# Third block of a decoder: compression, compressed scores, recurrence and convolution norm between the input projection's tiles

## What is computed

```
z = rms_norm(x) @ w_in            # 2848 columns: q, kc, vc, ks, vs, kw, vw, gates, conv, gla
kc, vc = compress(kc), compress(vc)     # 31 overlapping blocks of 32 tokens: silu(flat @ w1 + b1) @ w2
y_nsa  = g0*attn(q, kc, vc) + g1*attn(q, ks, vs) + g2*attn(q, kw, vw)      # 8 heads, 2 kv heads
y_conv = silu(layer_norm(causal depthwise conv of 31 taps (a * sigmoid(g))))
y_gla  = rms_norm(chunked gated linear attention (8 chunks of 64)) * silu(gr)
x = x + [y_nsa, y_conv, y_gla] @ w_out  # then feed-forward and embedding
```

## Time and profile before

| | |
|---|---|
| median of three executions | 2480.53 us (2477.56 to 2482.07) |
| the profiled execution, its own time | 2478.39 us |
| its span in the trace | 2476.6 us |
| PE, DVE, ACT, POOL busy | 2323.7, 1197.3, 913.4, 836.7 us |
| mean granted TensorE clock | 0.963 |

### The profile page before, as it was taken

How to read it: one execution, slowest core, us unless ns; L and a number is a source line. 1 busy time by engine, 2 the same in 40 slices (tenths; PEclk the granted TensorE clock), 3 DMA queues, 4 the chain that set the end, 5 groups by cost and what they waited for, 6 DMA issues and landing times.

```text
span 2476.6 us, 26005 instructions
## 1 busy us (share of the span) xinstructions
PE 2323.7 (94%) x10172; PEld 1784.8 (72%) x10172; DVE 1197.3 (48%) x2159; ACT 913.4 (37%) x1465; POOL 836.7 (34%) x328
## 2 busy tenths in 40 slices
PE   6999899999999899999999999999879899999997
PEld 4666678887877565557888878778774468888876
DVE  4444575553256565653655542447327553333124
ACT  3455443332233544543334322332217333222232
POOL 2222244444433111113444444344310034444442
PEclk9999999999999999999999999999759789999998
DMA  7111133333222101102332322253210023333222
GB/s 255 51 52 47 52 98 100 96 94 105 93 83 83 54 30 35 39 26 78 95 101 94 98 97 96 85 166 101 74 43 1 1 68 94 101 95 107 94 90 77
DMA packets 58347, 201.03 MB, mean 81 GB/s; under 512 B 6416, under 2 KB 10016, under 8 KB 58224
## 3 DMA queue, kind: packets, MB, share of 16 engines
q1 hardware_dynamic: 55360, 194.94, 24.8%
q10 hardware_dynamic: 2864, 4.40, 0.5%
HBM read 197.19 MB, written 7.38 MB: 83 GB/s over the span
## 4 chain that ended last, share of the span: by engine, by line
PE 81%; DVE 8%; ACT 6%; issue 2%; DMA 2%; SPq 0%; POOL 0%; ACTq 0%; DVEq 0%; PEldq 0%
PE lin L439 22%; PE lin L441 22%; PE lin L440 22%; PE lin L780 2%; DVE arena L1382 1%; PE scores L701 1%; PE obank L723 1%; PE turn L536 1%; ACT arena L1709 1%; PE lin L455 1%; PE obank L621 1%; PE lin L457 1%; PE lin L456 1%; PE scores L705 1%; PE scores L852 1%
## 5 line engine op out<-in xcount | busy, mean ns | idle before, releaser
L2076 POOL TENSOR_TENSOR w_lo<-slots,w_hi 128x1024 fp32r<-128x1024 f32 (+3 forms) x322 | 834.2, 2592 | 1483.6 <-ACT w_hi L1665 1483.3
L1665 ACT ACTIVATE w_hi<-slots 128x1024 fp32r<-128x1024 f32 (+3 forms) x322 | 357.4, 1110 | 705.4 <-DMA slots<-in_w_ffn_in 275.6
L439 PE MATMUL lin<-g_hi,w_hi 128*128 128x512 f32 x1416 | 561.4, 396 | 8.9 <-DVE arena L1114 8.2
L441 PE MATMUL lin<-g_hi,w_lo 128*128 128x512 f32 x1416 | 552.4, 390 | 0.0
L440 PE MATMUL lin<-g_lo,w_hi 128*128 128x512 f32 x1416 | 552.3, 390 | 0.0
L439 PEld LDWEIGHTS lin<-g_hi,w_hi 128*128 128x128 f32 x1416 | 266.6, 188 | 80.0 <-issue 24.3
L440 PEld LDWEIGHTS lin<-g_lo,w_hi 128*128 128x128 f32 x1416 | 266.8, 188 | 58.7 <-issue 3.8
L441 PEld LDWEIGHTS lin<-g_hi,w_lo 128*128 128x128 f32 x1416 | 266.6, 188 | 55.8
L439 PE MATMUL lin<-f_hi,w_hi 128*128 128x512 f32 x528 | 208.7, 395 | 4.0 <-DVE f_lo L1055 4.0
L1011 DVE TENSOR_TENSOR h<-lin,h 128x512 f32<-128x512 f32 x72 | 49.7, 691 | 328.7 <-PE lin L441 321.0
L441 PE MATMUL lin<-f_hi,w_lo 128*128 128x512 f32 x528 | 208.5, 395 | 0.0
(11 more groups left out here) (387 smaller groups left out, 3539.9 us busy)
## 6 DMA issues: line engine op xcount, KB each, us to landing
slots<-in_w_ffn_in SPq DMA_DIRECT2D x132, 512.0 KB, 3.4
slots<-in_w_ffn_out SPq DMA_DIRECT2D x48, 704.0 KB, 4.0
slots<-in_w_ple SPq DMA_DIRECT2D x24, 640.0 KB, 3.8
slots<-in_w_a_qkv SPq DMA_DIRECT2D x24, 512.0 KB, 3.5
slots<-in_w_c_in SPq DMA_DIRECT2D x23, 512.0 KB, 3.5
slots<-in_w_b_wo SPq DMA_DIRECT2D x16, 512.0 KB, 3.4
slots<-in_w_b_pair SPq DMA_DIRECT2D x8, 768.0 KB, 4.2
slots<-in_w_a_wo SPq DMA_DIRECT2D x16, 256.0 KB, 2.6
```

What stands on the lines that cost most here:

```text
L439: pe.matmul(lin[:, parity, :], hi, x_hi, start=k == 0, stop=False)
L441: mm = pe.matmul(lin[:, parity, :], lo, x_hi, start=False, stop=k == len(rhs) - 1)
L1665: ac.activation(w_hi[:, slot, at_], slots[:, slot, at_], ACT.Copy).then_inc(q.hi_made, 1)
L2076: po.tensor_tensor(w_lo[:, slot, at_], slots[:, slot, at_], w_hi[:, slot, at_].bitcast(F32), ALU.subtract).then_inc(q.weights_split, 1)
```

## The change

The four stages' barriers go; everything of stages 2 to 4 except the head loop is laid between projection tiles 9 to 22, and the rest behind the last.

- Order: `C_IN` brings the recurrence's inputs forward (tiles 9 to 12) and the value tiles to the end.
- Compression: the 62 columns of blocks are stationary and the unsplit fp32 weights (four chunks of 128 x 256 a group) move, 32 fp32 matmuls instead of 128 of high and low part, into one PSUM bank of 62 x 512, a group behind each of tiles 9 to 16. The hidden layer is then transposed (four transposes). The weights leave the ring: SP loads them into three buffers of their own (`load_cmp`), so ACT and POOL no longer split them.
- DVE: the block additions stand behind tiles 5 to 8, taps are spread by a table over tiles 3 to 16, then decay, updates, states, compressed softmax, norms behind tiles 11 to 22. PSUM copies of the recurrence move from DVE to ACT.
- PE: the recurrence's outputs between and within chunks are accumulated in one bank, so the four additions on DVE go. Compressed scores alternate the two kv halves.
- Output: chunks are reordered (recurrence and convolution first); their highs and lows are made in and behind the head loop, and `c_out` follows the last head product.

```diff
-C_IN = [14, 15, 12, 13, 8, 9, 10, 11, 22, 6, 7, 18, 19, 16, 17, 20, 21, 4, 5, 0, 1, 2, 3]
+C_IN = [14, 15, 12, 13, 8, 9, 10, 11, 22, 16, 17, 18, 19, 0, 1, 2, 3, 20, 21, 4, 5, 6, 7]
+CMP_FIRST, CMP_GROUPS, CMP_CHUNKS = 9, 8, 4
...
+            def load_cmp(m):
+                if m == 0:
+                    sp.wait_ge(q.p_split, 4)
+                    sp.wait_ge(q.tile_done, TILE["ple1"])
+                if m >= 3:
+                    sp.wait_ge(q.cmp_done, m - 2)
...
+                if name == "c_in" and k in (3, 4, 6, 13, 14, 15, 16, 17):
+                    load_cmp((3, 4, 6, 13, 14, 15, 16, 17).index(k))
...
-            for k in range(8):
-                w = weights("c_cmp", k)
...
-                for c in range(8):
-                    for x in range(2):
-                        mm = pe.matmul(lin[:, t % 2, 0:2 * NCMP], w[x][:, c * P:(c + 1) * P].bitcast(F32),
-                                       c_zp[:, k // 4, 8 * (k % 2) + c, :], start=c == 0 and x == 0,
-                                       stop=c == 7 and x == 1)
...
+            def compress(m):
+                kind = m // 4
+                pe.wait_ge(q.zp_made, 8 * (kind + 1))
+                pe.wait_ge(cmp_in[m % 3], 16 * (1 + m % 3 // 2) * (m // 3 + 1))
+                for c in range(CMP_CHUNKS):
+                    chunk = CMP_CHUNKS * (m % 4) + c
+                    mm = pe.matmul(obank[0:2 * NCMP, kind * HID:(kind + 1) * HID], c_zp[:, kind, chunk, :],
+                                   cmp_weights(m, c), start=chunk == 0, stop=chunk == 15)
+                mm.then_inc(q.cmp_done, 1)
...
+            for j in range(23):
...
+                if j == 9:
+                    gates_and_decay()
+                if CMP_FIRST <= j < CMP_FIRST + CMP_GROUPS:
+                    compress(j - CMP_FIRST)
+                if j == 15:
+                    within_chunks()
+                if j == 16:
+                    turned_gv()
+                if j == 17:
+                    hidden_turned()
+                    updates()
+                if j == 18:
+                    keys_and_values_compressed()
+                    conv_sums()
+                if j == 19:
+                    compressed_scores()
+                if j == 20:
+                    conv_squares()
+                    recurrence_out()
+                if j == 21:
+                    recurrence_sums(0)
+                if j == 22:
+                    turned_v(0)
+                    recurrence_sums(1)
...
+            taps_after = {3: 3, 4: 5, 5: 3, 6: 3, 7: 3, 8: 3, 9: 6, 10: 5, 11: 5, 12: 6, 13: 4, 14: 6, 15: 6, 16: 4}
...
+                if 5 <= j <= 8:
+                    blocks(j - 5)
...
+            recurrence_normed(0)
+            recurrence_normed(1)
...
-            end_stage(ve, 4)
-            out_lows(DC + BH, low, c_o_hi, c_o_lo, range(DC))
+            c_output(2)
+            c_lows(range(6))
+            c_output(3)
+            c_lows((6, 7))
...
+                if j == 22:
+                    load_p(2)
+                    copied_v(0)
+                    inv_sqrt(gl_e[:, 1, :], GV, q.gl_ss, q.gl_log, q.gl_fac, 2, 2)
+                    for x in range(2):
+                        ac.wait_ge(q.ln_norm, x + 1)
+                        ac.activation(low[:, x, :], c_acc[:, x, :], ACT.Silu, bias=v1("ln_b", x)).then_inc(q.gl_silu, 1)
+                    ac.preload_act_table_set("natural_log_exp_and_others")
...
+                if s == 3:
+                    ac.wait_ge(q.gl_norm, 4)
+                    ac.wait_ge(q.gl_silu, 4)
+                    c_highs(0, 1, 2, 3)
+                if s in (5, 7):
+                    c_pair_highs((s - 5) // 2)
```

More of the change, by code:

```diff
@@ L759, in _ @@
             mix = parts(c_mix_hi, c_mix_lo, DC)
[L760 to L769 removed]
+            banks = (scores[:, 0, :], scores[:, 1, :], turn[:, 0, :], turn[:, 1, :])
@@ new lines, in gates_and_decay @@
+            def gates_and_decay():
+                pe.wait_ge(q.extra_in, 16 * 4)
+                pe.wait_ge(q.tile_taken, TILE["c_in"] + 9)
+                pe.matmul(scores[:, 1, :], walpha[32:48, :], c_z[32:48, 22, :], start=True, stop=True).then_inc(q.gl_alpha, 1)
+                pe.wait_ge(q.r_ready, NORM["mix2"] + 1)
+                for k in range(NQ):
+                    mm = pe.transpose(stat[:, k * P:(k + 1) * P], c_z[:, 22, k * P:(k + 1) * P], ident)
+                mm.then_inc(q.gates_turned, 1)
@@ new lines, in conv_sums, with conv_squares @@
+            def conv_sums():
+                pe.wait_ge(q.conv_step, 2 * CW)
+                pe.wait_ge(q.gl_kdc, 1)
+                for x in range(2):
+                    mm = pe.matmul(stat[:, :], ones, c_acc[:, x, :], start=x == 0, stop=x == 1)
+                mm.then_inc(q.ln_summed, 1)
+            def conv_squares():
+                pe.wait_ge(q.ln_sq, 2)
+                for x in range(2):
+                    mm = pe.matmul(stat[:, :], ones, ln_s[x][:, :], start=x == 0, stop=x == 1)
+                mm.then_inc(q.ln_summed, 1)
@@ new lines, in recurrence_sums @@
+            def recurrence_sums(x):
+                pe.wait_ge(q.gl_sq, x + 1)
+                pe.wait_ge(q.ln_logged, 1)
+                wait(pe, q.gl_log, x)
+                pe.matmul(stat[:, :], ones64, gl_s[:, x, :], start=True, stop=True).then_inc(q.gl_ss, 1)
+            for j in range(23):
+                t = TILE["c_in"] + j
+                if j == 0:
+                    first_tile("mix2", "c_in", mix)
+                else:
+                    tile(t, t % 2, weights("c_in", j), 0, mix)
+                if j == 9:
[22 more added lines that the diff above has]
+                    recurrence_sums(1)
@@ L886, in _ @@
-            mm.then_inc(q.ln_summed, 1)
-            pe.wait_ge(q.gl_kdc, 3)
-            pe.wait_ge(q.gl_attc, 4)
-            for n in range(NCH):
-                rows = slice(64 * (n % 2), 64 * (n % 2) + 64)
-                b = (scores[:, 0, :], scores[:, 1, :])[n % 2]
-                if n >= 2:
-                    pe.wait_ge(q.gl_uc, 4 * (n - 1))
-                mm = pe.matmul(b[:, 0:2 * P], gl_kdt[rows, n // 2, :], gl_vt[rows, n // 2, :], start=True, stop=True)
-                mm.then_inc(q.gl_u, 1)
@@ L920, in _ @@
[L920 to L921 removed]
+            output_products("c_out", DC + BH, list(zip(c_o_hi, c_o_lo)))
             ffn_products(2)
@@ new lines, in _ @@
+                if j == 16:
+                    for x in range(2):
+                        ac.wait_ge(q.gl_kdt, 2 + x)
+                        ac.activation(gl_vt[:, :, x * P:(x + 1) * P], turn[:, x, :].rearrange("p (j c) -> p j c", c=P), ACT.Copy)\
+                            .then_inc(q.gl_kdc, 1)
+                if j == 17:
+                    ac.wait_ge(q.cc_turned, 1)
+                    for k in range(4):
+                        ac.activation(c_hid[:, k, :], obank[:, k * 2 * NCMP:(k + 1) * 2 * NCMP], ACT.Silu,
+                                      bias=v1("cmp_b1", k)).then_inc(q.hid_act, 1)
```

653 lines of the change are left out of this document (339 added, 314 removed).

## The result

The changed kernel takes 2386.38 us, the median of four runs (2385.04 to 2395.98), against 2481.3 for the kernel before in its four: ratio 0.9628, 95% interval 0.9601 to 0.9656. Faster, as forecast; 2393 was predicted, with 2374 to 2416 as range. The profiled execution took 2385.04 us (span 2383.3) at a mean granted clock of 0.987 (before: 0.963). Profile against profile the gain is 93.3 us, where the sum had 86.4.

What follows compares the result with a forecast made beforehand. It took PE work at half clock plus a serial tail as the bound; 143.9 us gone less 57.5 added (43.9 of it PE work between tiles) gave a gain of 86.4, so 2393 us, range 2374 to 2416.

Steps and rivals of the forecast that it cites:

- Compression 15.4: Compression between projection tiles: 64 records of 0.24 us at full clock, 15.4 us; bounds 14.6 and 30.8.
- rival 3: Clock falls at the first compression group and stays down: +108 us, 2501, slower than before; chance 0.03.
- Recurrence output 5.9: Recurrence output between tiles at full clock: 3.7 us plus 2.2 for the within-chunk products, 5.9 in all.
- Compressed scores 5.0, updates 3.8, the small products and transposes: PE work between tiles at full clock: scores between 6.5 and 3.6 us, updates 16 records of 0.24, small products 1.8.
- PE stall 2, from DVE: Near the bias band, DVE slowed beside POOL's subtractions makes PE wait 2 us; bounds 0 and 12.
- Rival 1: DVE becomes the projection's bound, held wholly by POOL's subtractions: about 10 us, 2403; chance 0.15.
- One clock dip, 3: Near tiles 19 and 20, one clock fall to 0.50 over dense tiles costs 3 us; bounds 0 and 25.
- Rival 2: Clock falls for late tiles only, at scores, recurrence output and tiles behind: +25 less 3 counted, 2415; chance 0.12.
- a few more: A head loop beginning at full clock instead of 0.50 could gain a few us beyond the lower end, 2383.
- Head loop's start 6.6 behind the bias's old place: After the last tile, ACT's table loads and Silu delay the heads' first exponential: 6.6 us added.
- The tail 47.4 and the output's half clock 2.0: Last head copy to first output matmul, 47.4 us, goes whole; ten output matmuls at full clock save 2.0 us.
- Rival 4: Waits on DVE or ACT in the state and score chain, tiles 17 to 21, hold PE: +30, 2423; chance 0.08.

Runs made afterwards that it cites:

- e1: Against the changed kernel, compression with the unsplit weights stationary and the 62 block columns moving, still between the tiles; 2390.9 us.
- e2a: Against the changed kernel, the recurrence output's 16 products of 128 rows come first, then its 32 within-chunk products of 64 rows; 2377.1 us.
- e8: Against the changed kernel, compressed scores run all of one kv half, then all of the other, instead of alternating; 2394.5 us.
- e5: Against the changed kernel, three of the four chunks of every compression group left out, weights still loaded; 2382.8 us.
- e9: Against the changed kernel, three quarters of the compression and 448 of the 512 columns of 42 convolution taps left out; 2379.5 us.
- e7: Against the changed kernel, ACT's six early roundings for the output projection moved from the head loop to behind it; 2389.2 us.
- e4: Against the changed kernel, the first three compression weight loads issued with the weights of tiles 9 to 11 instead of 3, 4 and 6; 2388.8 us.
- e2b: As e2a, but the within-chunk products alternate between the two row halves of the array from one to the next; 2380.6 us.
- e3: Against the changed kernel, ACT's two Silu with their table loads put ahead of the value copy and second recurrence factor; 2388.4 us.

## Why the prediction was right, point by point

The forecast held, with a sum 6.9 us short of the gain. One term was off by as much, and others in the opposite direction. The stage from the first to the last take grew by 51.1 us: inserts (the work laid between the tiles) 43.3, their seams 2.2, stall 1.3 with 1.5 of half clock behind it, dips at tiles 20 and 21 2.8. The sum is measured; where an insert ends and its seam begins is known to a few tenths.

- *Compression 15.4*: 15.0, at full clock. Its upper end, 30.8, and rival 3 are out, for 62 stationary columns and, by e1, for 62 moving ones.
- *Recurrence output 5.9*: 12.9. This is the mis-sized term. The step that failed is costing the two kinds of products each from rows in which they ran by themselves; in the change they take turns, which costs 0.62 us for one large product and its two small ones instead of 0.29, and the clock falls in the middle. e2a shows both: by kind it is 4.7, below the forecast.
- *Compressed scores 5.0, updates 3.8, the small products and transposes*: 3.7, 1.9, and for the rest 4.0 less together. For the scores the ratio of the head scores, 3.6, was the right end, and the mean of the two ends the wrong choice (e8). So 43.9 against 43.3 is luck: +7.0 in one term and -7.6 in the others cancel.
- *PE stall 2, from DVE*: 1.3 more stall than before at tile 7 and 1.5 of half clock behind it, but from late weights. DVE did slow down beside POOL (four block additions took 8.23 us at tile 7, where 0.59 each was counted), and never reached PE. Rival 1 did not occur, but it is near: e5 and e9 show DVE holding PE once PE has 11.2 us less to do.
- *One clock dip, 3*: 2.8, from two in the projection's end, 1.6 at tile 20 and 1.2 at tile 21; another 3.0 is inside the 12.9 of the recurrence output. Rival 2 had the places nearly right (the scores themselves ran at 1.00) and its 25 us far too much.
- *ACT in the head loop 2*: 0, by e7. *The loop's clock*: 88.6 us before, from the first exponential to the last head copy, and 84.3 now; these 4.3 us are what the sentence on the lower end called "a few more" and did not count. The mean granted clock is 0.92 over the loop before (line below), in which it began at 0.50, and 0.98 now; e4, whose loop had 0.92 again by two dips, took 87.6. So up to some 3 of the 4.3 us hang on where the dips fall: luck, and not a sure gain.

```profile
1854.40:1943.00 88.60, 82.41 (x459) 39.47 (x457) 58.30 (x258) 62.45 (x200) 0.00 (x0) 0.92 0.00 1
```

- *Head loop's start 6.6 behind the bias's old place*: 5.9, the same chain as foretold: copy, factor, table load, Silu, table load.
- *The tail 47.4 and the output's half clock 2.0*: the tail went whole, and the output and the rest gained 4.3 (481.9 us from the first output matmul to the end). In the twelve other kernels this same code took 482.6 to 483.6, so 0.7 to 1.7 of it is luck too.
- Rival 4 did not occur: behind tile 7 PE waits for nobody until the last take.

## What to carry to other kernels

Narrow matmuls that run at half clock by themselves can cost half when they are laid between dense tiles in short pieces, whichever operand stands: here the compression's 1.7 to 1.9 us never lowered the clock, and the scores' 3.7 and the recurrence output's 12.9 did, the scores in five kernels of thirteen, the output in all nine that kept its order. Before laying work there, add up the other engines tile by tile, since taking work off the full engine gains nothing where the next one is a step behind. Order small products by kind, so that no full-array product stands between two small ones: here that was 8.2 us for an exchange of loops, 3.0 of them half clock that went with it. How neighbours lie in the array matters too (e2b, e8). When edits are worth a few us, compare them by stage within the traces, because the same code ahead of them moved by 8 us from run to run.

## What the runs showed of the hardware that I had not expected

- A pair of 128x128 records and four 64x64 ones in turns: 0.62 us; by kind 0.22 + 0.07. The price is at the change of kind. A dense record next to an insert also starts 0.1 us late on either side.
- 64x64 records of 64 columns went at 0.017 us each when every change of product went to the other column half and every second one to the other row half too, and at 0.023 when every one went to the other row half and nearly all kept the columns.
- The clock fell although PE was busy 3.90 of 3.90 (compressed scores) and 4.80 of 4.80 (recurrence output): being busy with narrow records was not enough to keep it. But the same scores left it at 1.00 in eight of the thirteen changed kernels (e3 and e4 among them), and so did the recurrence output where it was done in 4.7 us (e2a).
- Stalls of 2.1 to 3.4 us at tile 7 were each followed by some 3 us at 0.50 in the changed kernels, and the 2.14 us of the kernel before were not. No run explains this difference.
